# One load, one exponential and one signal per chunk instead of four, in the prompt's state scan

## The chip, the cores and the metric

The kernel runs on one core of a Trainium2 chip. The metric is the device time of one execution in microseconds. Three runs of the kernel before took 2939.79, 2950.26 and 2951.13 us; their median is 2950.26 us. The profile was taken of one execution of 2939.79 us.

## The reference, cut to what matters

The program is one inference step of a decoder layer: latent attention and a Mamba-2 scan side by side, then a mixer that gathers expert rows. The change lies in the scan over the prompt (512 tokens, 32 heads of 64 channels in 4 groups, state size 128), which goes in 4 chunks of 128 tokens:

```python
def step(h, inp):
    xc, dtc, bc, cc = inp
    acs = jnp.cumsum(dtc * a_gr, axis=1)
    seg = acs[:, :, None] - acs[:, None, :]
    decay = jnp.exp(jnp.where(causal[None, :, :, None, None], seg, -jnp.inf))
    cb = jnp.einsum('bign,bjgn->bijg', cc, bc)
    w = cb[..., None] * decay * dtc[:, None]
    y_diag = jnp.einsum('bijgr,bjgrp->bigrp', w, xc)
    y_off = jnp.einsum('bign,bgrpn->bigrp', cc, h) * jnp.exp(acs)[..., None]
    to_end = jnp.exp(acs[:, -1:] - acs) * dtc
    h_new = jnp.exp(acs[:, -1])[..., None, None] * h + jnp.einsum('bjgn,bjgr,bjgrp->bgrpn', bc, to_end, xc)
    return h_new, y_diag + y_off
```

So a chunk needs, for each of 32 heads, a 128 x 128 matrix of decays, and the state that the chunk before left.

## The kernel before, in words

The program is a row of stages, one function each. Each stage has its own block of five engine programs, whose order is the order of the code; engines wait for one another by counting semaphores, and a barrier ends a block. `prompt_scan` is one such stage. It does two things at once.

The first is the scan. The cumulative sums `acs` (32 heads x 512 tokens) lie in device memory. For each chunk c they are loaded to the tile `ce`, [128 partitions, 32 heads, 128 tokens], every partition getting the same values: 2 MB, in rows of 512 B. From then on:

- VectorE (DVE), L1260: `seg` = min(`ce` − `acs_tok`, 0), 32 instructions, one per head.
- ScalarE (ACT), L1224: `seg` = exp(`seg`); L1226 and L1227 two small ones; L1230: `ce` = exp(`ce`).
- DVE, L1267: `cb`, the masked products of B and C, then L1273: `seg` = `seg` * dt * `cb`, 32 instructions; L1280: `ce` = `ce` * C (not in chunk 0, which has no state before it).
- TensorE (PE), L1183 and L1185: Y of a head from `x_tok` and `seg`, and from `state` and `ce`. After each group of eight heads PE raises `summed`.
- DVE, L1287: `xw`; L1292: adds the skip term to Y; L1298 and L1303: the new state, from PE's products L1191.

`ce` is read by PE until the last product of its group of heads is summed; then ACT issues the load of the next chunk's values (L1236). The first chunk's load is issued by SyncE (L1135). All of these go in four quarters of eight heads (q or g from 0 to 3), each with its own load, wait and signal.

The second thing is filler: 16 products of 128 columns of a weight with all tokens, the gates (`gates(n)`, four per chunk), each 48 matmuls. SyncE loads a weight chunk, GpSimd (POOL) rounds it (L372), DVE makes the rest `w_lo` (L348), PE multiplies (L354 to L356), ACT drains the bank (L1209) and stores it (L1211). On PE two gate products stand between the first products of a chunk (`cb`) and Y, one between Y and the state's products L1191, one after these. Tokens and `cb` of the next chunk follow (L1166, L1170).

Of the kernel before, what the change touches and what calls it, by code (L numbers as in the profile page):

```python
# [19 lines left out]
ALU = mybir.AluOpType  # L20
ACT = mybir.ActivationFunctionType
# [3 lines left out]
P = 128  # L25
# [12 lines left out]
DI, HD, SH, G, N = 2048, 64, 32, 4, 128  # L38
# [1032 lines left out]
def prompt_scan(nc, A, K, S, h_hi, h_lo, proj, acs_dram, outs):  # L1071
# [4 lines left out]
    HP = SH // G  # L1076
    GATES = 2 * D // P
    EACH = GATES // TT
    with ExitStack() as ctx:
        m = Mem(nc, ctx, "scn")  # L1080
# [9 lines left out]
        seg, ce = m.sb("seg", [P, SH, P]), m.sb("ce", [P, SH, P])  # L1090
# [3 lines left out]
        state_out = xw[:, 0:1024].rearrange("p (b n) -> p b n", b=2)  # L1094
        to_end, end = m.sb("to_end", [P, SH]), m.sb("end", [P, SH])
        bank = [m.ps(f"bank{b}", [P, 512]) for b in range(4)]
        read_in = [m.sem(f"read_in{q}") for q in range(4)]
        turned, copied, cb_made = m.sem("turned"), m.sem("copied"), m.sem("cb_made")
        cb_masked, seg_made, decayed, exped, weighted = (m.sem(n) for n in ("cb_masked", "seg_made", "decayed", "exped", "weighted"))
        ce_made, x_weighted, summed, y_done, grown, state_done = (m.sem(n) for n in ("ce_made", "x_weighted", "summed", "y_done", "grown", "state_done"))  # L1100
        end_exped, end_in, chain = m.sem("end_exped"), m.sem("end_in"), m.sem("chain")
# [28 lines left out]
        @block.sync  # L1130
        def _(sp):
            columns = chunks_from(IN - 2 * D, GATES)
            weights_in(sp, w, w_view, w_in, lowered, columns, 0, 2)
            for q in range(4):
                sp.dma_start(heads_of(ce, q), acs_all[:, q * HP:(q + 1) * HP, 0:P].to_broadcast([P, HP, P])).then_inc(read_in[q], 16)  # L1135
            weights_in(sp, w, w_view, w_in, lowered, columns, 2, GATES)
            for q in range(4):
                sp.wait_ge(out_copied, q + 1)
                sp.dma_start(outs["ssm_p"][0, 0].rearrange("(k a) p n -> (a p) k n", a=2)[:, 4 * q:4 * q + 4, :],
                             state_out[:, q % 2, :].rearrange("p (k n) -> p k n", k=4)).then_inc(stored[q % 2], 16)  # L1140
            sp.wait_ge(stored[0], 32)
            sp.wait_ge(stored[1], 32)
# [59 lines left out]
        @block.scalar  # L1202
        def _(act):
            def drain(n):

                act.wait_ge(multiplied, n + 1)
                if n >= 2:
                    act.wait_ge(out_stored[n % 2], 16 * (n // 2))
                act.activation(out[:, n % 2].rearrange("p (s t) -> p s t", s=2), ps[:, n % 2, :, 0:HALF], ACT.Copy).then_inc(drained, 1)  # L1209
                act.wait_ge(drained, n + 1)  # L1210
                act.dma_start(proj[C_GA + n], out[:, n % 2]).then_inc(out_stored[n % 2], 16)  # L1211

            for c in range(TT):

                for q in range(5):
                    act.wait_ge(turned, 5 * c + q + 1)
                    if c and q == 0:
                        act.wait_ge(summed, 4 * c)
                        act.wait_ge(x_weighted, c)
                        act.wait_ge(grown, 4 * c)  # L1220
                    act.activation(x_tok[:, q * 512:(q + 1) * 512] if q < 4 else b_tok[:, :], bank_of(c, TOKENS + q)[:, :], ACT.Copy).then_inc(copied, 1)
                for q in range(4):
                    act.wait_ge(seg_made, 4 * c + q + 1)
                    act.activation(heads_of(seg, q), heads_of(seg, q), ACT.Exp).then_inc(decayed, 1)  # L1224
                act.wait_ge(end_in, c + 1)
                act.activation(to_end[:, :], to_end[:, :], ACT.Exp).then_inc(end_exped, 1)  # L1226
                act.activation(end[:, :], ce[:, :, P - 1], ACT.Exp).then_inc(end_exped, 1)  # L1227
                act.wait_ge(end_exped, 2 * c + 2)
                for q in range(4):
                    act.activation(heads_of(ce, q), heads_of(ce, q), ACT.Exp).then_inc(exped, 1)  # L1230
                drain(EACH * c)
                drain(EACH * c + 1)
                if c + 1 < TT:
                    for q in range(4):
                        act.wait_ge(summed, 4 * c + q + 1)
                        act.dma_start(heads_of(ce, q), acs_all[:, q * HP:(q + 1) * HP, (c + 1) * P:(c + 2) * P].to_broadcast([P, HP, P])).then_inc(read_in[q], 16)  # L1236
                drain(EACH * c + 2)
                drain(EACH * c + 3)
            for b in range(2):
                act.wait_ge(out_stored[b], 16 * (GATES // 2))  # L1240

        @block.vector
        def _(dve):
# [10 lines left out]
            lower_to(2)  # L1254
            for c in range(TT):
                at = slice(c * P, (c + 1) * P)
                for q in range(4):
                    dve.wait_ge(read_in[q], 16 * c + 16)
                    for h in range(8 * q, 8 * q + 8):
                        last = dve.tensor_scalar(seg[:, h, :], ce[:, h, :], S["acs_tok"][:, c, h:h + 1], 0.0, ALU.subtract, ALU.min)  # L1260
                    last.then_inc(seg_made, 1)
                dve.tensor_tensor(to_end[:, :], ce[:, :, P - 1], S["acs_tok"][:, c, :], ALU.subtract).then_inc(end_in, 1)
                lower_to(EACH * c + 3)
                dve.wait_ge(cb_made, c + 1)
                if c:
                    dve.wait_ge(weighted, 4 * c)
                dve.tensor_tensor(cb[:, :, :], bank_of(c, CB)[:, :].rearrange("p (g i) -> p g i", g=G),  # L1267
                                  K["keep"][:, :].rearrange("p (a i) -> p a i", a=1).to_broadcast([P, G, P]), ALU.mult).then_inc(cb_masked, 1)
                dve.wait_ge(cb_masked, c + 1)
                for q in range(4):  # L1270
                    dve.wait_ge(decayed, 4 * c + q + 1)
                    for h in range(8 * q, 8 * q + 8):
                        last = dve.scalar_tensor_tensor(seg[:, h, :], seg[:, h, :], S["dt_tok"][:, c, h:h + 1], cb[:, h // HP, :], ALU.mult, ALU.mult)  # L1273
                    last.then_inc(weighted, 1)
                    if q == 2:
                        lower_to(EACH * c + 4)
                if c:
                    for g in range(G):
                        dve.wait_ge(exped, 4 * c + g + 1)
                        dve.tensor_tensor(heads_of(ce, g), heads_of(ce, g),  # L1280
                                          S["x"][:, XC_ + g:XC_ + g + 1, at].to_broadcast([P, HP, P]), ALU.mult).then_inc(ce_made, 1)
                else:
                    dve.sem_inc(ce_made, G)
                dve.wait_ge(end_exped, 2 * c + 2)
                then(dve.tensor_tensor(to_end[:, :], to_end[:, :], S["dt_tok"][:, c, :], ALU.mult))
                dve.wait_ge(copied, 5 * c + 4)
                dve.tensor_tensor(xw[:, :].rearrange("p (h d) -> p h d", h=SH), x_tok[:, :].rearrange("p (h d) -> p h d", h=SH),  # L1287
                                  to_end[:, :].rearrange("p (h a) -> p h a", a=1).to_broadcast([P, SH, HD]), ALU.mult).then_inc(x_weighted, 1)
                for q in range(4):
                    dve.wait_ge(summed, 4 * c + q + 1)  # L1290
                    for k in range(4 * q, 4 * q + 4):
                        last = dve.scalar_tensor_tensor(S["x"][:, k, at], S["x"][:, k, at], S["skip"][:, k:k + 1],  # L1292
                                                        bank_of(c, Y + q)[:, (k % 4) * P:(k % 4 + 1) * P], ALU.mult, ALU.add)
                    last.then_inc(y_done, 1)
                lower_to(EACH * c + 5)
                view = lambda ap: ap.rearrange("p (h d) -> p h d", d=HD)
                if c:
                    then(dve.tensor_tensor(view(state[:, :]), view(state[:, :]),  # L1298
                                           end[:, :].rearrange("p (h a) -> p h a", a=1).to_broadcast([P, SH, HD]), ALU.mult))
                for g in range(G):  # L1300
                    dve.wait_ge(grown, 4 * c + g + 1)
                    part, new = state[:, g * 512:(g + 1) * 512], bank_of(c, GROWTH + g)[:, :]
                    (dve.tensor_tensor(part, part, new, ALU.add) if c else dve.tensor_copy(part, new)).then_inc(state_done, 1)  # L1303
                lower_to(EACH * c + 6)
# [1336 lines left out]
```

## Time and profile before

| what | before |
|---|---|
| median of three runs | 2950.26 us |
| the profiled execution | 2939.79 us |
| its span in the trace | 2937.8 us |
| busy, share of the span | PE 85%, DVE 70%, POOL 48%, ACT 30% |

The span is from the first to the last instruction of the profiled execution. The busy share of an engine is an average over stages with different limits. The prompt's scan lies between about 475 and 660 us of the span; a timeline lists the instructions of one engine in order of time there, and in brackets how long the engine had stood idle before one, and what released it. In waits, "issue" means that the profile shows nothing that the engine waited for.

### The profile page before, as it was taken

How to read it: one execution, taken by the hardware profiler on the slowest of the kernel's cores; microseconds unless marked ns; L12 is line 12 of the kernel's file. 1: busy time of each engine (PE TensorE's matmuls, PEld its weight loads, DVE VectorE, ACT ScalarE, POOL GpSimd, SP SyncE). 2: the span in 40 equal slices, each digit the busy share in tenths (PEclk: the TensorE clock that was granted, in tenths of full speed). 3: DMA queues.
4: the chain of work that ended last, by engine and by line, in shares of the span. 5: the costliest groups of instructions: out<-in, count | busy, mean ns of one | idle time of the engine just before them, and what ended most of it. 6: DMA issues, size and time to landing. Idle time of an engine off the chain costs nothing.

```text
span 2937.8 us, 36561 instructions
## 1 busy us (share of the span) xinstructions
PE 2486.9 (85%) x11667; PEld 1705.1 (58%) x11667; DVE 2054.1 (70%) x4001; ACT 885.7 (30%) x3576; POOL 1400.3 (48%) x1162
## 2 busy tenths in 40 slices
PE   3898997984998997887999999999999999846823
PEld 1898996873455563444666556565556565524810
DVE  3575686975460111498898989898989798976577
ACT  2232002314150000223454445454444444410110
POOL 0211232200000000287778788877787787765475
PEclk7899998997999998898999999999999999956555
DMA  4333575436006641699999999999999999999588
GB/s 152 99 97 109 177 219 165 127 89 201 15 1 186 223 140 64 240 398 393 373 345 394 337 395 352 381 362 376 377 356 381 357 370 360 384 356 379 204 314 322
DMA packets 372174, 776.19 MB, mean 264 GB/s; under 512 B 47250, under 2 KB 178323, under 8 KB 371946
## 3 DMA queue, kind: packets, MB, share of 16 engines
q0 software_dynamic: 154144, 562.17, 51.0%
q1 hardware_dynamic: 196714, 187.06, 19.9%
q10 hardware_dynamic: 21124, 24.63, 2.6%
q8 instruction: 93, 1.52, 0.2%
q14 instruction: 99, 0.80, 0.1%
HBM read 744.46 MB, written 29.50 MB: 263 GB/s over the span
## 4 chain that ended last, share of the span: by engine, by line
issue 25%; POOL 11%; DVE 8%; PE 8%; DMA 7%; ACT 1%; SPq 0%; POOLq 0%; DVEq 0%; ACTq 0%
POOL mix_v L2012 5%; POOL mix_u L2003 5%; DMA mix_u<-in_peer_u,mix_ids 4%; DVE mix_u L2485 3%; DVE mix_acc L2390 3%; PE mix_pair L2179 2%; PE mix_pair L2038 1%; DMA smp_w_out<-in_peer_keys 1%; PE mix_pair L2070 1%; PE mix_pair L2150 1%; PE mix_pair L2093 1%; PE mix_pair L2157 0%; DMA pag_kpe<-in_cache_kpe 0%; PE mix_pair L2085 0%; ACT L2288 0%
## 5 line engine op out<-in xcount | busy, mean ns | idle before, releaser
L2070 PE MATMUL mix_pair<-pag_wx,pag_ckvT 128*128 128x384 f32 (+3 forms) x3072 | 968.2, 462 | 14.4 <-ACT mix_raw L2252 9.4
L2485 DVE CUSTOM_DVE_ANT_0 mix_u<-mix_u,mix_h 128x1024 f32<-128x1024 f32 x512 | 623.3, 1217 | 216.7 <-DMA mix_u<-in_peer_u,mix_ids 214.6
L2012 POOL DMA_INDIRECT mix_v<-in_peer_v,mix_ids x512 | 644.1, 1258 | 224.3 <-issue 157.8
L2070 PEld LDWEIGHTS mix_pair<-pag_wx,pag_ckvT 128*128 128x128 f32 x3072 | 565.7, 192 | 304.8 <-issue 33.0
L2003 POOL DMA_INDIRECT mix_u<-in_peer_u,mix_ids x512 | 599.5, 1171 | 256.2 <-issue 147.7
L2390 DVE SCALAR_TENSOR_TENSOR mix_acc<-mix_v,mix_coef,mix_acc 128x1024 f32<-128x1024 f32 x449 | 575.1, 1281 | 0.0
L2250 ACT ACTIVATE mix_pair<-mix_pair 128x128 f32<-128x128 f32 x1024 | 267.1, 261 | 230.1 <-PE mix_pair L2070 229.3
L2085 PE MATMUL mix_pair<-mix_v,mix_diag 128*128 128x512 f32 x236 | 128.6, 672 | 103.7 <-ACT mix_diag L2267 102.7
L1988 POOL IOTA mix_count_i<- 128x16 int32 x1 | 0.1, 134 | 452.6 <-POOLq L88 452.6
L2259 ACT ACTIVATE mix_coef<-mix_dots 128x4 f32<-128x4 f32 x128 | 26.3, 205 | 550.8 <-DVE mix_dots L2485 550.8
L2250 ACT ACTIVATION_READ_ACCUMULATOR mix_pair<-mix_pair 128x1 f32 x1024 | 189.9, 185 | 0.0
L354 PE MATMUL stp_ps<-inp_h_hi,stp_w_hi 128*128 128x260 f32 x512 | 148.4, 290 | 17.3 <-DVE stp_w_lo L348 17.3
L356 PE MATMUL stp_ps<-inp_h_hi,stp_w_lo 128*128 128x260 f32 x512 | 146.3, 286 | 0.0
L355 PE MATMUL stp_ps<-inp_h_lo,stp_w_hi 128*128 128x260 f32 x512 | 145.9, 285 | 0.0
L1663 DVE TENSOR_TENSOR mrg_gate<-mrg_psB,mrg_gate 128x520 f32<-128x520 f32 x8 | 5.6, 699 | 197.4 <-PE mrg_psB L1624 197.4
L2085 PEld LDWEIGHTS mix_pair<-mix_v,mix_diag 128*128 128x128 f32 x236 | 47.9, 211 | 153.7 <-issue 82.5
L354 PE MATMUL cnv_ps<-inp_h_hi,cnv_w_hi 128*128 128x260 f32 x416 | 120.6, 290 | 0.0
L356 PE MATMUL cnv_ps<-inp_h_hi,cnv_w_lo 128*128 128x260 f32 x416 | 118.2, 284 | 0.0
L355 PE MATMUL cnv_ps<-inp_h_lo,cnv_w_hi 128*128 128x260 f32 x416 | 117.8, 283 | 0.0
L1624 PE MATMUL mrg_psB<-frt_x,mrg_wb 128*128 128x260 f32 x512 | 114.2, 384 | 0.0
L2038 PE MATMUL mix_pair<-chs_h2T,chs_wq 128*128 128x512 f32 x256 | 113.1, 600 | 0.4 <-ACT chs_h2T L2223 0.4
L354 PEld LDWEIGHTS stp_ps<-inp_h_hi,stp_w_hi 128*128 128x128 f32 x512 | 98.2, 192 | 19.3 <-DVE stp_w_lo L348 19.2
(480 smaller groups left out, 4210.9 us busy)
## 6 DMA issues: line engine op xcount, KB each, us to landing
pag_ckv<-in_cache_ckv SPq DMA_DIRECT2D x128, 256.0 KB, 14.8
stp_w<-in_w_in SPq DMA_DIRECT2D x32, 512.0 KB, 4.7
mrg_w_ada<-in_w_ada SPq DMA_DIRECT2D x8, 2048.0 KB, 8.2
cnv_w<-in_w_in SPq DMA_DIRECT2D x26, 512.0 KB, 3.5
keep_proj<-stp_out ACTq DMA_DIRECT2D x32, 260.0 KB, 2.8
ada_w_ada<-in_w_ada SPq DMA_DIRECT2D x4, 2048.0 KB, 11.3
stp_st<-in_state_ssm POOLq DMA_DIRECT2D x8, 1024.0 KB, 6.9
out_ssm_s<-stp_st POOLq DMA_DIRECT2D x8, 1024.0 KB, 6.9
```

What stands on the lines that cost most here:

```text
L354: pe.matmul(out, w_hi, x_hi, start=first, stop=False)
L355: pe.matmul(out, w_hi, x_lo, start=False, stop=False)
L356: return pe.matmul(out, w_lo, x_hi, start=False, stop=last)
L1624: last = pe.matmul(psB[:, b, s, 0:HALF], wb[:, b, k, :], yT[:, k, s * HALF:(s + 1) * HALF], start=(k == 0), stop=(k == KI - 1))
L2003: pool.indirect_dma_start(u[:, x % UR, :], None, u_rows, bass.IndirectOffsetOnAxis(at, 0)).then_inc(u_in[x % UR], 16)
L2012: pool.indirect_dma_start(v[:, y % VR, :], None, v_rows, bass.IndirectOffsetOnAxis(at, 0)).then_inc(v_in[y % VR], 16)
L2038: last = pe.matmul(bank[2 + side][:, :], wq[:, h % 2, k, side * P:(side + 1) * P], h2T[:, k, :], start=(k == 0), stop=(k == KD - 1))
L2070: last = pe.matmul(to, ckvT[:, g % 2, k, :], wx[:, k, lo:hi], start=(k == 0), stop=(k == KL - 1))
L2085: last = pe.matmul(psV[:, c, :], diag[:, d % 2, :], v[:, r, c * 512:(c + 1) * 512], start=(x == first_on_pe[t]), stop=(x == last_on_pe[t]))
L2250: last = act.activation(psN[j][:, at:at + NOPE], psN[j][:, at:at + NOPE], ACT.Square, accum_out=ss[:, b % 2, t, h:h + 1])
L2390: dve.scalar_tensor_tensor(acc[:, :], v[:, r, :], c, acc[:, :], ALU.mult, ALU.add).then_inc(v_used[r], 1)
L2485: dve.tensor_tensor_reduce(u[:, r, :], u[:, r, :], h2[:, t % 2, :], 1.0, 0.0, ALU.mult, ALU.add, dots[:, t % 2, slot:slot + 1]).then_inc(u ...
```

## The change

The quarters of the loads, of the first signal and of the exponentials become one each. The weighting L1273 and the products L1280 are still signalled to PE by groups of eight heads.

```diff
-        read_in = [m.sem(f"read_in{q}") for q in range(4)]
-        turned, copied, cb_made = m.sem("turned"), m.sem("copied"), m.sem("cb_made")
+        read_in, turned, copied, cb_made = m.sem("read_in"), m.sem("turned"), m.sem("copied"), m.sem("cb_made")
...
-            for q in range(4):
-                sp.dma_start(heads_of(ce, q), acs_all[:, q * HP:(q + 1) * HP, 0:P].to_broadcast([P, HP, P])).then_inc(read_in[q], 16)
+            sp.dma_start(ce[:, :, :], acs_all[:, :, 0:P].to_broadcast([P, SH, P])).then_inc(read_in, 16)
...
-                for q in range(4):
-                    act.wait_ge(seg_made, 4 * c + q + 1)
-                    act.activation(heads_of(seg, q), heads_of(seg, q), ACT.Exp).then_inc(decayed, 1)
+                act.wait_ge(seg_made, c + 1)
+                act.activation(seg[:, :, :], seg[:, :, :], ACT.Exp).then_inc(decayed, 1)
...
-                for q in range(4):
-                    act.activation(heads_of(ce, q), heads_of(ce, q), ACT.Exp).then_inc(exped, 1)
+                act.activation(ce[:, :, :], ce[:, :, :], ACT.Exp).then_inc(exped, 1)
...
-                    for q in range(4):
-                        act.wait_ge(summed, 4 * c + q + 1)
-                        act.dma_start(heads_of(ce, q), acs_all[:, q * HP:(q + 1) * HP, (c + 1) * P:(c + 2) * P].to_broadcast([P, HP, P])).then_inc(read_in[q], 16)
+                    act.wait_ge(summed, 4 * c + 4)
+                    act.dma_start(ce[:, :, :], acs_all[:, :, (c + 1) * P:(c + 2) * P].to_broadcast([P, SH, P])).then_inc(read_in, 16)
...
-                for q in range(4):
-                    dve.wait_ge(read_in[q], 16 * c + 16)
-                    for h in range(8 * q, 8 * q + 8):
-                        last = dve.tensor_scalar(seg[:, h, :], ce[:, h, :], S["acs_tok"][:, c, h:h + 1], 0.0, ALU.subtract, ALU.min)
-                    last.then_inc(seg_made, 1)
+                dve.wait_ge(read_in, 16 * c + 16)
+
+                for h in range(SH):
+                    last = dve.tensor_scalar(seg[:, h, :], ce[:, h, :], S["acs_tok"][:, c, h:h + 1], 0.0, ALU.subtract, ALU.min)
+                last.then_inc(seg_made, 1)
...
+                dve.wait_ge(decayed, c + 1)
                 for q in range(4):
-                    dve.wait_ge(decayed, 4 * c + q + 1)
...
                 if c:
+                    dve.wait_ge(exped, c + 1)
                     for g in range(G):
-                        dve.wait_ge(exped, 4 * c + g + 1)
```

On ACT this is what stands in chunk 0 before, from the exponential of `seg` to the reload of `ce` for chunk 1. In brackets is the semaphore that the instruction waits for:

```order
L1224 ACTIVATE scn_seg<-scn_seg 128x1024 [waits scn_seg_made] x4
L1226 ACTIVATE scn_to_end<-scn_to_end 128x32 [waits scn_end_in]
L1227 ACTIVATE scn_end<-scn_ce 128x32
L1230 ACTIVATE scn_ce<-scn_ce 128x1024 [waits scn_end_exped]
L1230 ACTIVATE scn_ce<-scn_ce 128x1024 x3
L1209 ACTIVATE scn_out<-scn_ps 128x520 [waits scn_multiplied]
L1211 DMA keep_proj<-scn_out 128x520 [waits scn_drained]
L1209 ACTIVATE scn_out<-scn_ps 128x520 [waits scn_multiplied]
L1211 DMA keep_proj<-scn_out 128x520 [waits scn_drained]
L1236 DMA scn_ce<-keep_acs 128x8x128 [waits scn_summed] x4
```

And in the changed kernel, whose lines have other numbers:

```order
L1221 ACTIVATE scn_seg<-scn_seg 128x4096 [waits scn_seg_made]
L1223 ACTIVATE scn_to_end<-scn_to_end 128x32 [waits scn_end_in]
L1224 ACTIVATE scn_end<-scn_ce 128x32
L1226 ACTIVATE scn_ce<-scn_ce 128x4096 [waits scn_end_exped]
L1207 ACTIVATE scn_out<-scn_ps 128x520 [waits scn_multiplied]
L1209 DMA keep_proj<-scn_out 128x520 [waits scn_drained]
L1207 ACTIVATE scn_out<-scn_ps 128x520 [waits scn_multiplied]
L1209 DMA keep_proj<-scn_out 128x520 [waits scn_drained]
L1231 DMA scn_ce<-keep_acs 128x32x128 [waits scn_summed]
```

Each row of four is one row of four times the size. The single load waits until all four groups of heads are summed.

On DVE, the differences of chunk 1 and what follows them up to the first weighting, before:

```order
L1260 TENSOR_SCALAR scn_seg<-scn_ce,frt_acs_tok 128x128 [waits scn_read_in0]
L1260 TENSOR_SCALAR scn_seg<-scn_ce,frt_acs_tok 128x128 x7
L1260 TENSOR_SCALAR scn_seg<-scn_ce,frt_acs_tok 128x128 [waits scn_read_in1]
L1260 TENSOR_SCALAR scn_seg<-scn_ce,frt_acs_tok 128x128 x7
L1260 TENSOR_SCALAR scn_seg<-scn_ce,frt_acs_tok 128x128 [waits scn_read_in2]
L1260 TENSOR_SCALAR scn_seg<-scn_ce,frt_acs_tok 128x128 x7
L1260 TENSOR_SCALAR scn_seg<-scn_ce,frt_acs_tok 128x128 [waits scn_read_in3]
L1260 TENSOR_SCALAR scn_seg<-scn_ce,frt_acs_tok 128x128 x7
L1262 TENSOR_TENSOR scn_to_end<-scn_ce,frt_acs_tok 128x32
L348 TENSOR_TENSOR scn_w_lo<-scn_w,scn_w_hi 128x1024 [waits scn_rounded]
L1267 TENSOR_TENSOR scn_cb<-scn_bank,frt_keep 128x512 [waits scn_weighted,scn_cb_made]
L1273 SCALAR_TENSOR_TENSOR scn_seg<-scn_seg,frt_dt_tok,scn_cb 128x128 [waits scn_decayed,scn_cb_masked]
```

The same place in the changed kernel:

```order
L1255 TENSOR_SCALAR scn_seg<-scn_ce,frt_acs_tok 128x128 [waits scn_read_in]
L1255 TENSOR_SCALAR scn_seg<-scn_ce,frt_acs_tok 128x128 x31
L1257 TENSOR_TENSOR scn_to_end<-scn_ce,frt_acs_tok 128x32
L348 TENSOR_TENSOR scn_w_lo<-scn_w,scn_w_hi 128x1024 [waits scn_rounded]
L1262 TENSOR_TENSOR scn_cb<-scn_bank,frt_keep 128x512 [waits scn_weighted,scn_cb_made]
L1268 SCALAR_TENSOR_TENSOR scn_seg<-scn_seg,frt_dt_tok,scn_cb 128x128 [waits scn_decayed,scn_cb_masked]
L1268 SCALAR_TENSOR_TENSOR scn_seg<-scn_seg,frt_dt_tok,scn_cb 128x128 x23
```

DVE's instructions keep their number, size and order; only the waits moved, to the first of 32.

## Rows read from the trace of the kernel before

**Rows 1.** Waits, 470 to 665 us: who waited for what, us in total, times, longest.
```profile
PE scn_bank L1183 <- issue: 10.9, 1, 10.9
DVE scn_state L1303 <- PE scn_bank L1191: 9.8, 13, 3.6
DVE scn_seg L1260 <- DMA scn_ce<-keep_acs: 7.1, 4, 2.5
```

**Rows 2.** Timeline of DVE, chunk 0: start, us, line, op, tiles, [idle before].
```profile
495.30 1.66 DVE L1260 TENSOR_SCALAR scn_seg<-scn_ce,frt_acs_tok 128x128 f32<-128x128 f32 x8 [2.18 <-DMA scn_ce<-keep_acs]
...
500.70 0.68 DVE L1267 TENSOR_TENSOR scn_cb<-scn_bank,frt_keep 128x512 f32<-128x512 f32 x1
501.42 6.44 DVE L1273 SCALAR_TENSOR_TENSOR scn_seg<-scn_seg,frt_dt_tok,scn_cb 128x128 f32<-128x128 f32 x24
```

**Rows 3.** Timeline of DVE, chunks 1 to 3.
```profile
526.64 8.00 DVE L1260 TENSOR_SCALAR scn_seg<-scn_ce,frt_acs_tok 128x128 f32<-128x128 f32 x32
...
536.53 6.39 DVE L1273 SCALAR_TENSOR_TENSOR scn_seg<-scn_seg,frt_dt_tok,scn_cb 128x128 f32<-128x128 f32 x24
...
546.86 4.62 DVE L1280 TENSOR_TENSOR scn_ce<-scn_ce,frt_x 128x1024 f32<-128x1024 f32 x4
...
568.26 8.07 DVE L1260 TENSOR_SCALAR scn_seg<-scn_ce,frt_acs_tok 128x128 f32<-128x128 f32 x32
...
608.42 8.07 DVE L1260 TENSOR_SCALAR scn_seg<-scn_ce,frt_acs_tok 128x128 f32<-128x128 f32 x32
```

**Rows 4.** Timeline of PE: first product of Y, and first gate product after.
```profile
513.84 0.58 PE L354 MATMUL scn_ps<-inp_h_hi,scn_w_hi 128*128 128x260 f32 x1
...
548.33 0.70 PE L1183 MATMUL scn_bank<-scn_seg,scn_x_tok 128*64 128x128 f32 x4 [2.75 <-DVE scn_ce L1280]
...
557.01 0.39 PE L354 MATMUL scn_ps<-inp_h_hi,scn_w_hi 128*128 128x260 f32 x1
...
575.46 0.37 PE L354 MATMUL scn_ps<-inp_h_hi,scn_w_hi 128*128 128x260 f32 x1
...
590.03 0.45 PE L1183 MATMUL scn_bank<-scn_seg,scn_x_tok 128*64 128x128 f32 x4 [2.82 <-DVE scn_ce L1280]
...
597.19 0.39 PE L354 MATMUL scn_ps<-inp_h_hi,scn_w_hi 128*128 128x260 f32 x1
```

**Rows 5.** Loads of ce: chunk 1's first, its fourth, chunk 0's four; issue, landing.
```profile
L1236 ACTq DMA_DIRECT2D scn_ce<-keep_acs x1: 377/377/377, 551.9 to 551.9; - x1
DMA to landing us min/median/max: 5.6/5.6/5.6
...
L1236 ACTq DMA_DIRECT2D scn_ce<-keep_acs x1: 1839/1839/1839, 557.1 to 557.1; - x1
DMA to landing us min/median/max: 12.2/12.2/12.2
...
L1135 SPq DMA_DIRECT2D scn_ce<-keep_acs x4: 875/2058/4145, 476.0 to 481.1; - x4
DMA to landing us min/median/max: 7.8/11.6/14.2
```

**Rows 6.** Exponentials: timeline of ACT, and L1224 by ns min/median/max.
```profile
534.20 3.93 ACT L1224 ACTIVATE scn_seg<-scn_seg 128x1024 f32<-128x1024 f32 x4
...
L1224 ACT ACTIVATE scn_seg<-scn_seg x16: 1056/1089/1096, 485.5 to 618.8; 128x1024 f32<-128x1024 f32 x16
```

**Rows 7.** DMA issues of the page: KB each, median us to landing.
```profile
mrg_w_ada<-in_w_ada SPq DMA_DIRECT2D x8, 2048.0 KB, 8.2
```

**Rows 8.** Timeline of PE, in an earlier stage.
```profile
253.52 0.59 PE L354 MATMUL stp_ps<-inp_h_hi,stp_w_hi 128*128 128x260 f32 x1 [9.31 <-DVE stp_w_lo L348]
```

**Rows 9.** Windows: length, busy PE, PEld, DVE, ACT, POOL; PEclk; DMA; GB/s.
```profile
253.00:258.00 5.00, 4.48 (x21) 4.48 (x22) 2.69 (x4) 1.48 (x3) 2.28 (x2) 0.51 0.58 165
258.00:263.00 5.00, 5.00 (x44) 5.00 (x43) 4.93 (x3) 0.60 (x1) 1.17 (x2) 1.00 0.16 48
```

**Rows 10.** Timeline of ACT, drain of a gate product in chunk 1.
```profile
563.09 0.60 ACT L1209 ACTIVATE scn_out<-scn_ps 128x520 f32<-128x520 f32 x1 [16.86 <-PE scn_ps L356]
```

## The prediction

> **What bounds the kernel now.** The page's busy shares come first (they are in the table of the profile above): over the whole run no engine is full, so the shares say nothing of one stage. The change lies in one stage, the prompt's state scan, which the timelines put at about 475 to 660 us; so I read that stretch alone, first its waits, then the order in time of VectorE (DVE), TensorE (PE) and ScalarE (ACT).
>
> The waits [rows 1] show that DVE waits little: 7.1 us for the loads of `ce`, all in the first chunk, and 9.8 us for PE's state products. PE waits 10.9 us once (chunk 0) and then at most 2.8 us per chunk, until DVE has made `ce`. DVE's timeline says the same: the decay differences (L1260) start at 526.64, 568.26 and 608.42 [rows 3], so a chunk takes 41.6 and 40.2 us, and in between DVE is nearly never idle. The ring that sets the end of the stage is therefore: differences, weighting (L1273), `ce` times C (L1280) on DVE; then Y (L1183/L1185), a gate product and the state products on PE; then the state on DVE; then the next differences. The exponentials on ACT and the reload of `ce` by DMA lie beside this ring. What must be seen is how much room each of them has.
>
> *The reload.* In chunk 1 four quarters are issued, as each group of heads is summed: the first at 551.9, to land 5.6 us later, at 557.5, the fourth at 557.1, to land 12.2 us later, at 569.3 [rows 5]. So they arrive one every 3.93 us. The first reader starts at 568.26 with no wait, and needs the fourth quarter only 6 us later. *The exponentials.* Four pieces of 1024 take 3.93 us together, from 534.20 [rows 6], while DVE is still at the differences and at other work; the weighting starts at 536.53, about 1.9 us after the last difference (526.64 + 8.00) [rows 3].
>
> **The change part by part.** It computes the same; each group of four (loads, difference signals, exponentials) becomes one. Instructions on DVE and PE are the same ones in the same order. What changes is when they may start.
>
> *a) Exponential of `seg` after all 32 differences (four times).* It can only begin when the 32nd difference is done, and no weighting can begin until all of it is done. Chunk 0: the fourth group of differences begins at 495.30, since the fourth quarter lands there [rows 2]. One load of the same bytes lands at the same moment, and then all 32 differences stand behind it: 8.00 us [rows 3], to 503.3. The exponential: I take the 3.93 us of the four (bounds: 3.6, if three fixed parts go, and 4.4 for four times the single 1.09) [rows 6], to 507.2. The weighting started at 501.42, so chunk 0 is late by 5.8 us. In chunks 1 to 3, once the differences have started, it costs 8.00 + 3.93 − (536.53 − 526.64) = 2.0 us each. DVE's other work there (`to_end`, a w_lo and the mask of `cb`, the 1.9 us between 534.64 and 536.53) fits below the 3.93.
>
> *b) Reload of `ce` after the last sum, in one transfer (three times).* The load is issued when Y ends, not after its first quarter. Its length is not in the trace: no 2 MB load with this source was run. From the quarters: first one 5.6, three more at 3.93, so 5.6 + 11.8 = 17.4 us. Upper bound: in chunk 0 the four, issued together, took from 476.0 to 481.1 + 14.2, 19.3 us, with weights ahead of them [rows 5]. Lower bound: the 2 MB loads of w_ada land in 8.2 us [rows 7]. I take 17.4, since it is the same source, destination and row of 512 B, and the four already ran back to back.
>
> *c) PE's clock.* PE will stand before each Y. The row nearest to what comes is the 9.31 us idle before 253.52 [rows 8]: granted clock 0.51 (1.2 GHz) for the next 5 us, then 1.00 [rows 9]. Of 4.48 us of work at half clock half is lost, 2.2 us. Y takes 7.2 us at full clock (590.03 to 597.19) [rows 4], so 9.4 us here. Bounds: no loss, or all of Y at half clock, 14.4.
>
> The sum, chunk by chunk:
> - Chunk 0: +5.8. Y ended at 513.84 [rows 4], now 519.6; the load lands at 537.0. DVE started at 526.64 and is ready at 532.4, so the start is +10.4; plus 2.0 by (a), weighting is at +12.4.
> - Chunk 1: Y starts at 548.33 + 12.4 = 560.7, ends at 570.1; `ce` lands at 587.5, where DVE began at 568.26: +19.2, weighting +21.2.
> - Chunk 2: Y starts at 590.03 + 21.2 = 611.2, ends 620.6; `ce` lands at 638.0, where DVE began at 608.42: +29.6, weighting +31.6.
> - Chunk 3: no reload. For Y's slower start +0.5 (0 if its clock had fallen before as well, as in chunk 1, where Y took 8.7 us; 2.2 if not). The rest of the stage follows as before.
>
> Together +32 us. By this, the ring becomes Y 9.4, load 17.4, differences 8.1, exponential 3.9, weighting and first `ce` product about 11.8 (536.53 to 548.33): 50.6 us where it was 41.6 and 40.2.
>
> *What costs nothing.* The `exped` wait: ACT's pass over `ce` has the size of that over `seg`, so it ends some 4.4 us after it (two small ones between); DVE's weighting takes 10.3 (536.53 to 546.86) [rows 3], so 5.9 us of cover are left. Fewer launches on ACT: it is idle for 16.86 us before its next drain [rows 10]. ACT's queue when it issues 2 MB: the fourth quarter held it for 1.84 us, as transfers stood ahead of it [rows 5]; one big issue may hold ACT for 7 us or so, at worst until the load has landed. Behind it waits the drain of gate chunk 4c+2, which before came 6.1 us after Y's end (563.09 against 557.01) [rows 4, 10], and whose bank PE wants only at 575.46, 18.4 us after Y's end; so up to 17.4 us nothing is late, and ACT's copies after that have slack until the differences are done. The three or four weight loads and the stores queue as before; the store of 4c+2 goes behind the load, and ACT asks for it only after the next exponentials. Nothing outside the stage is touched: the stages are parted by barriers.
>
> *Two rules against these rows.* The quarters carry 512 KB per 3.93 us, 133 GB/s [rows 5]. The Trainium skill ("DMA: Bandwidth & Descriptors", section Bandwidth, Measured) says to batch loads to at least 1 MiB, and its formula of 2.0 us plus bytes over 436 GB/s would give an estimated 6.8 us for the 2 MB; by that the reload would not be seen and the sum would be near +6. The trace disagrees: the three later quarters, already queued, came no faster than 3.93 us each. A rule of the Trainium skill that speaks against the change ("Perfetto Trace Analysis", Optimizing Scalar/DVE Operations): where ScalarE is not saturated but causes bubbles on others, smaller instructions may let work end sooner; grouping saves about 93 ns each. Here grouping would give back an estimated 1.1 us in all (4 × 3 × 93 ns), against +32.
>
> **The rivals.**
> 1. *The big load is quick: no measurable change.* A single transfer might run at the rate of the w_ada loads, 8.2 us [rows 7]. Then `ce` is there before DVE asks; the point from which this decides is 568.26 − 557.01 = 11.3 us (12.8 in chunk 0). Chunk 0 would gain what the earlier load gives, but the mask of `cb` stands behind a w_lo and begins at 500.70 [rows 2], so about 0; chunks 1 to 3 keep 2.0 each by (a): +6. For it: 512 KB in 3.93 us is half the rate of those loads, so there is room above it. Against it: the spacing of queued quarters. Between the ends, each us by which the load is under 17.4 takes off 3 us.
> 2. *PE stays at half clock through all of Y.* For it: after only 2.75 us of standing Y took 8.7 us in chunk 1 (548.33 to 557.01), against 7.2 in chunk 2 after 2.82 [rows 4]. Price: 14.4 − 9.4 = 5.0 us in each of chunks 1 to 3, as the load is issued only at Y's end: +15, so +47. The same time would come of a load that is 5 us slower beside the weights. Against it: 253 to 263, where dense work brought the clock back.
> 3. *The big load is a little quicker: +15 to +25.* In one piece it lands in 12 to 15 us, three times 2.4 to 5.4 us sooner.
>
> **How the numbers follow.** The profiled execution took 2939.8 us (span 2937.8); the median of the runs is 2950.3, so 10.5 above. With +32 it would be 2971.8, and against the median 2982.3. Forecast 65%, own range +26 to +39 (exponential −1 to +2, load from 15.4 to 19.3, clock −5 to +2), so 2976 to 2989. Rival 2: 13%, 2997. Rival 1: 11%, 2956. Rival 3: 8%, 2965 to 2975. Something that I don't see, 3%, faster. The runs of before lie 11 us apart, so I set the range from 2962 to 3000. What can be told from no change is about 0.5%, 15 us. Slower by more: forecast, rivals 2 and 3: 0.85. Same: rival 1 and the edge of 3: 0.12. Faster: 0.03.
>
> **What would show it.** In the changed profile: one load of `ce` per chunk that lands about 17 us after the end of Y; DVE waiting for it 4.6 us in chunk 1 and about 6 us in chunks 2 and 3; one exponential of 4096 in about 3.9 us, and the weighting starting right after it; PE standing 9 to 11 us before each Y, at granted clock 0.5 for the next 4 to 5 us; starts of the differences some 50 us apart; nothing moved in the later stages beyond a shift. I am wrong if the load lands within 11 us, if the weighting starts before the whole exponential, or if another stage changes by more than 5 us.

## The result and the profile after

| | before | after |
|---|---|---|
| median of the runs | 2950.7 us (4) | 2983.4 us (4) |
| profiled execution / its span | 2939.8 / 2937.8 us | 2975.7 / 2973.8 us |
| the stage | 188.1 us | 219.3 us |

The ratio of the runs is 1.0118 (the two medians alone give 1.0111), 95% interval 1.0098 to 1.0139: slower by 29 to 41 us of 2951. Forecast were +32 us and 2982. "The stage" is here, and in all of what follows, the time from PE's first product of the prompt's scan to the next stage's table load on ACT: 474.99 to 663.08 before, 476.95 to 696.25 after. The stage began 1.96 us later after the change, so times of after are compared with before less 1.96. The stage grew by 31.2 us; of the span's 36.0 the other 4.8 lie before and behind it (2.0 and 2.8), where both kernels are the same.

The timeline of DVE after the change, at the differences and the weighting of each chunk, answers to [rows 2, 3]:

```profile
496.67 8.07 DVE L1255 TENSOR_SCALAR scn_seg<-scn_ce,frt_acs_tok 128x128 f32<-128x128 f32 x32 [11.41 <-DMA scn_ce<-keep_acs]
508.51 7.17 DVE L1268 SCALAR_TENSOR_TENSOR scn_seg<-scn_seg,frt_dt_tok,scn_cb 128x128 f32<-128x128 f32 x24 [1.92 <-ACT scn_seg L1221]
538.60 8.07 DVE L1255 TENSOR_SCALAR scn_seg<-scn_ce,frt_acs_tok 128x128 f32<-128x128 f32 x32 [5.71 <-DMA scn_ce<-keep_acs]
550.45 7.20 DVE L1268 SCALAR_TENSOR_TENSOR scn_seg<-scn_seg,frt_dt_tok,scn_cb 128x128 f32<-128x128 f32 x24 [1.92 <-ACT scn_seg L1221]
589.63 7.82 DVE L1255 TENSOR_SCALAR scn_seg<-scn_ce,frt_acs_tok 128x128 f32<-128x128 f32 x32 [6.59 <-DMA scn_ce<-keep_acs]
601.23 7.17 DVE L1268 SCALAR_TENSOR_TENSOR scn_seg<-scn_seg,frt_dt_tok,scn_cb 128x128 f32<-128x128 f32 x24 [1.92 <-ACT scn_seg L1221]
640.47 8.00 DVE L1255 TENSOR_SCALAR scn_seg<-scn_ce,frt_acs_tok 128x128 f32<-128x128 f32 x32 [6.48 <-DMA scn_ce<-keep_acs]
652.25 6.39 DVE L1268 SCALAR_TENSOR_TENSOR scn_seg<-scn_seg,frt_dt_tok,scn_cb 128x128 f32<-128x128 f32 x24 [1.92 <-ACT scn_seg L1221]
```

Two new waits stand in each chunk: for the load before the differences, and 1.92 us for the exponential before the weighting. Between the last three starts of the differences lie 51.0 and 50.8 us, where it was 41.6 and 40.2. The loads in chunks 0 to 2, by issue and landing, answer to [rows 5]:

```profile
L1231 ACTq DMA_DIRECT2D scn_ce<-keep_acs x3: 377/378/380, 520.8 to 622.8; - x3
DMA to landing us min/median/max: 17.7/17.7/17.8
```

PE's first product of Y in chunks 1 to 3, with how long it stood, answers to [rows 4]:

```profile
562.28 0.70 PE L1181 MATMUL scn_bank<-scn_seg,scn_x_tok 128*64 128x128 f32 x4 [10.55 <-DVE scn_ce L1275]
...
613.03 0.70 PE L1181 MATMUL scn_bank<-scn_seg,scn_x_tok 128*64 128x128 f32 x4 [11.16 <-DVE scn_ce L1275]
...
663.26 0.70 PE L1181 MATMUL scn_bank<-scn_seg,scn_x_tok 128*64 128x128 f32 x4 [10.44 <-DVE scn_ce L1275]
```

The windows from there on in chunk 1 (the figure before the last two is the granted clock) answer to [rows 9]:

```profile
562.00:566.00 4.00, 3.72 (x36) 3.75 (x38) 4.00 (x5) 0.00 (x0) 3.39 (x1) 0.50 0.00 0
566.00:568.00 2.00, 2.00 (x31) 2.00 (x30) 1.97 (x2) 0.00 (x0) 0.37 (x1) 0.76 0.00 0
568.00:570.00 2.00, 2.00 (x42) 2.00 (x39) 2.00 (x7) 0.00 (x0) 0.00 (x0) 1.00 0.04 8
```

After 10.55 us of standing, some 5 us of Y run at half clock (1.2 GHz); Y lasts from 562.28 to the first gate product at 571.72, 9.44 us. In chunks 2 and 3 it lasts 9.65 and 8.46 us; before, the three took 8.68, 7.16 and 8.83.

### The profile page after: what moved, and what is told of

Its sections match the earlier page's. It is cut to its first block, busy times and chain, and to the rows that moved or that the text cites. A ratio compares the mean times of both kernels' runs of the same rounds, so it can differ in the third digit from the quotient of the medians.

```text
span 2973.8 us, 36525 instructions
## 1 busy us (share of the span) xinstructions
PE 2481.9 (83%) x11667; PEld 1702.0 (57%) x11667; DVE 2056.1 (69%) x4001; ACT 883.2 (30%) x3552; POOL 1386.6 (47%) x1162
## 4 chain that ended last, share of the span: by engine, by line
issue 26%; POOL 11%; DMA 9%; DVE 7%; PE 5%; ACT 1%; SPq 0%; POOLq 0%; DVEq 0%; ACTq 0%
DMA mix_u<-in_peer_u,mix_ids 6%; POOL mix_v L2007 6%; POOL mix_u L1998 5%; DVE mix_u L2480 3%; DVE mix_acc L2385 3%; PE mix_pair L2174 2%; PE mix_pair L2033 1%; DMA smp_w_out<-in_peer_keys 1%; PE mix_pair L2088 1%; PE mix_pair L2152 0%; DMA pag_kpe<-in_cache_kpe 0%; ACT L2283 0%; DMA mod_mul<-keep_ada 0%; PE mix_pair L2040 0%; DVE mix_rstd L2406 0%
```

## The experiments

Chips differ, and the rest of the program moves by more than most terms here (in the first four kernels that I changed, on a chip where the whole took some 3% longer, what follows the stage took 2367 to 2395 us). So the stage in the trace is what is compared. The third column leaves out chunk 0: it counts from the first weighting of chunk 0 to the end of the stage, because chunk 0 alone moved by 2 us between runs in which it was the same.

| kernel | stage, us | of it behind chunk 0's first weighting, us | ratio to before (95%) |
|---|---|---|---|
| before, twice | 188.1, 183.7 | 161.7, 158.9 | |
| changed, twice | 219.3, 219.0 | 187.7, 187.5 | 1.0118; 1.0115 (1.0084 to 1.0145) |
| exponentials whole | 193.1 | 167.5 | 1.0050 (1.0021 to 1.0079) |
| load whole | 213.8 | 184.2 | 1.0111 (1.0075 to 1.0147) |
| loads issued late | 190.6 | 166.2 | 1.0010 (0.9975 to 1.0046) |
| four loads, one wait | 211.8 | 181.5 | 1.0076 (1.0050 to 1.0102) |
| PE kept busy | 212.3 | 181.2 | 1.0076 (1.0051 to 1.0101) |
| other source | 200.4 | 169.2 | 1.0057 (1.0022 to 1.0091) |
| other pitch | 195.3 | 170.5 | one run |
| long rows, whole | 188.4 | 165.8 | 1.0017 (1.0002 to 1.0031) |
| long rows, quarters | 174.9 | 156.6 | 0.9973 (0.9957 to 0.9989) |

The kernel before and the changed one, run once more on one chip:

> The kernel before once more, for its trace on the same chip as the runs beside it. From the first product of the stage on PE to the next stage's table load on ACT it took 188.1 us; expected 188 to 190 us here.

> The changed kernel once more, beside the kernel before on the same chip: its stage took 219.3 us in the first trace, 31.2 us more than before. By the theory (the parts add up along the ring) the same 30 to 33 us here, wherever the rest of the program stands; if the loss depends on the chip or on the load of its memory, the load of ce lands more than 1 us away from 17.7 us.

The loads landed in 17.8 to 18.0 us and the changed stage took the same time within 0.3 us. The kernel before took 4.4 us less than in its first trace: 1.7 of it up to the first weighting of chunk 0, and 1.7 because Y ran into the half clock in one chunk and not in two: 8.62 us in chunk 2 there, 8.68 and 8.83 in chunks 1 and 3 in the first trace, at a granted clock of 0.57 to 0.62 in the first 4 us, and 7.16 at 1.00 in the others. So its stage is known to 4 us, and the loss is 31 to 35 us.

**The parts one by one.** First the exponentials alone: against the kernel before,

```diff
                 for q in range(4):
                     dve.wait_ge(read_in[q], 16 * c + 16)
...
-                    last.then_inc(seg_made, 1)
+                last.then_inc(seg_made, 1)
...
-                    act.wait_ge(seg_made, 4 * c + q + 1)
-                    act.activation(heads_of(seg, q), heads_of(seg, q), ACT.Exp).then_inc(decayed, 1)
+                act.wait_ge(seg_made, c + 1)
+                act.activation(seg[:, :, :], seg[:, :, :], ACT.Exp).then_inc(decayed, 1)
```

> The changed kernel with its loads in four quarters again, each issued and waited for as before; the differences are still signalled once and the two exponentials are one instruction each. Theory (the two parts of the change add up along the ring, each by its own wait): chunk 0 pays nothing, since the last difference ends at about 497.0, the exponential of 3.6 us ends at 500.6 and the mask of cb is not made before 501.4; chunks 1 to 3 pay 8.0 + 3.6 + 0.1 - 9.9 = 1.8 us each: +5.5 us, 2956 us. The weighting starts right after the exponential, with DVE idle 1.9 us before it. Rival (most of the loss is in the coarse exponential, for example because PE then stands and its clock falls): +15 us or more.

```profile
524.50 8.07 DVE L1258 TENSOR_SCALAR scn_seg<-scn_ce,frt_acs_tok 128x128 f32<-128x128 f32 x32
536.34 7.18 DVE L1271 SCALAR_TENSOR_TENSOR scn_seg<-scn_seg,frt_dt_tok,scn_cb 128x128 f32<-128x128 f32 x24 [1.92 <-ACT scn_seg L1223]
```

These are differences and weighting of chunk 1: 11.84 us apart, where it was 9.89. The stage took 193.1 us, +5.0 on the first trace of before (+9.4 on the second). The run times say more, +6 to +24 us; since the changed lines end with the stage, and what follows it differs by up to 27 us between kernels that are the same there, I go by the stage, and the rest of that ratio stays unexplained. Then the load alone, the change with its exponentials in quarters again:

> The changed kernel with the differences signalled and the exponentials done in four quarters again; the load stays whole. Theory: chunk 0 starts its differences when the whole load lands and its mask of cb follows them, +4.1 us; each reload lands 17.7 us after the end of Y: weighting at +9.0, +16.2, +25.0 us in chunks 1, 2, 3, so +25.5 us in all, 2976 us. DVE waits for the load 5 to 7 us in each of chunks 1 to 3. Rival (the coarse exponential carries the loss): under +15 us.

213.8 us, +25.8 against the 25.5 forecast; the load is the larger part. DVE waited 5.8, 7.8 and 7.4 us for it, a little over the 5 to 7 said, as the loads landed in 18.1 to 18.9 us on this chip. That 5.0 + 25.8 = 30.8 leaves only 0.4 of the 31.2 is in part chance, as the first weightings of chunk 0 show, here with the exponentials whole and then with the load whole:

```profile
501.79 6.39 DVE L1271 SCALAR_TENSOR_TENSOR scn_seg<-scn_seg,frt_dt_tok,scn_cb 128x128 f32<-128x128 f32 x24 [0.78 <-ACT scn_seg L1223]
...
507.47 6.39 DVE L1271 SCALAR_TENSOR_TENSOR scn_seg<-scn_seg,frt_dt_tok,scn_cb 128x128 f32<-128x128 f32 x24
```

From the start of the stage they come 0.9 us earlier and 3.2 us later than before, 2.3 together, where the change itself has 5.1: chunk 0 pays for the exponential only where the load is whole too. Behind that the two runs together have 5.9 + 22.5 = 28.4 us, where the change has 26.1. One reason is PE's clock, which the two parts don't pay twice: the three Y together take 27.7 us with the exponentials alone, 27.3 with the load alone and 27.6 with both, against 24.7 before; with the exponentials alone PE stood 3.9 to 4.7 us before each, and the granted clock began at 0.50 to 0.57.

**Which property of the load.** It was issued later, it was one transfer, and it had one wait. Against the kernel before, only issued later:

```diff
+                    act.wait_ge(summed, 4 * c + 4)
                     for q in range(4):
-                        act.wait_ge(summed, 4 * c + q + 1)
```

> The kernel before, but the four quarter loads of the next chunk are issued together after the last sum of Y, as late as the single load of the changed kernel; each still has its own semaphore and its own wait. Theory A (the loss comes from waiting for the last byte before the first difference): the first quarter lands 5.6 us after the end of Y, at 562.6, where DVE asks at 568.3; the fourth at 17.4 to 17.7, 574.5, where it is asked for at 574.3: +0 to +1 us, 2951 us. Theory B (the loss comes from issuing late, 5 us later than the first quarter was): about half of what the whole load cost, +10 to +20 us.

+2.5 us, within what before itself varies. The cover was thinner than counted: the timeline shows DVE waiting for a fourth quarter in each of chunks 1 to 3, 3.57 us at most,

```profile
500.96 6.45 DVE L1273 SCALAR_TENSOR_TENSOR scn_seg<-scn_seg,frt_dt_tok,scn_cb 128x128 f32<-128x128 f32 x24
...
568.58 4.87 DVE L1260 TENSOR_SCALAR scn_seg<-scn_ce,frt_acs_tok 128x128 f32<-128x128 f32 x24
577.02 1.66 DVE L1260 TENSOR_SCALAR scn_seg<-scn_ce,frt_acs_tok 128x128 f32<-128x128 f32 x8 [3.57 <-DMA scn_ce<-keep_acs]
```

but three quarters are worked on meanwhile, and the weighting comes 0.4, 2.0 and 0.4 us later after the first difference than before. The stage hides part of the price: chunk 0, which the edit doesn't touch, was 2.0 us shorter (first weighting at 500.96, 24.4 us into the stage, against 26.4). Behind it the stage took 4.6 us more than in the first trace of before and 7.3 more than in the second. So issuing late costs some 5 to 7 us: more than theory A's 0 to 1, less than theory B's 10 to 20. Now with the same four loads, and a wait for all of them first:

```diff
                 for q in range(4):
                     dve.wait_ge(read_in[q], 16 * c + 16)
+                for q in range(4):
                     for h in range(8 * q, 8 * q + 8):
```

> The kernel before, but the four quarter loads are issued together after the last sum of Y, and DVE waits for all four before its first difference; exponentials in quarters. It differs from the run that issued late only in the waits, and from the run with the whole load only in the size of the transfers. Theory (the wait for the last byte costs, not the size of the transfer): the stage takes as long as with the whole load, 213.8 us, within 2 us. Rival (one transfer of 2 MB is slower or faster than four of 512 KB): it differs by three times the difference, 5 us or more.

211.8 us: 21 us more than the run before it by the waits alone, 5.9 of them in chunk 0 and 15.3 behind it, and 2.1 from the run with one transfer, just over the 2 allowed and far from the rival's 5. So the loss by the load is mainly the wait for its last byte before the first difference; behind chunk 0 it is 15 of 20 to 23 us, and the late issue is the rest. The 2.1 us between one transfer and four are fewer than before itself varies by.

**PE's clock.** In the changed kernel, before Y in chunks 1 to 3:

```diff
+                if c:
+                    bank_free(pe, c, Y)
+                    for _i in range(80):
+                        pe.matmul(bank_of(c, Y)[:, 0:HALF], h_hi[:, 0, 0:P], h_hi[:, 0, 0:HALF], start=True, stop=True)
```

> The changed kernel with 80 matmuls of 128x260 more before Y in chunks 1 to 3, on fixed operands, into the bank that Y then overwrites: about 9.6 us of work at full clock in the 10.4 to 11.2 us that PE stood idle. Theory (c): Y starts at full clock and takes 7.2 us instead of 9.4 in each of the three chunks, all of it on the ring, so the stage falls from 219.2 us by 6 to 7, to 212.6. Rival 1 (the clock does not lie on the ring, since DVE's product of ce feeds Y no faster than 1.15 us a group): under 2 us. Rival 2 (the added matmuls end late and push Y): the stage grows.

212.3 us, 6.9 less. Y starts and ends, in chunk 1 of this kernel, at

```profile
559.52 0.45 PE L1185 MATMUL scn_bank<-scn_seg,scn_x_tok 128*64 128x128 f32 x4 [2.10 <-DVE scn_ce L1279]
...
566.68 0.39 PE L354 MATMUL scn_ps<-inp_h_hi,scn_w_hi 128*128 128x260 f32 x1
```

7.16 us for 9.44, and 7.16 in chunks 2 and 3 too, so the half clock at Y's start is on the ring and its price is that of the forecast. This is the price against a PE that never stands. Against the kernel before, whose Y ran into the half clock in two chunks of three, the three Y of the change took 27.6 us for 24.7: the clock accounts for 2.9 of the 31 us.

**Why the load takes 17.7 us.** First another source, in the changed kernel:

```diff
-                    act.dma_start(ce[:, :, :], acs_all[:, :, (c + 1) * P:(c + 2) * P].to_broadcast([P, SH, P])).then_inc(read_in, 16)
+                    act.dma_start(ce[:, :, :], A["w_in"][:, 0:P, 0:8192].rearrange("l p (h a n) -> p (l h) a n", a=2, n=P)[:, :, 0, :]).then_inc(read_in, 16)
```

> The changed kernel, but the three reloads of ce read rows of a weight matrix in place of acs: the same 4096 rows of 512 B to the same place, every partition from its own row, so that no source byte is read twice (chunks 1 to 3 compute with other numbers, and to_end takes its difference the other way round there). Theory A (the load is slow because all 128 partitions read the same 16 KB): it lands in 8 to 10 us after its issue, DVE does not wait for it, and what is left is chunk 0 and the exponentials, +11 us, 2962 us. Theory B (512 B rows through one queue go at about 3.9 us per 1024, whatever they read): it lands in 17.7 us and the time is 2983 us.

As many rows of 512 B came in 9.5 to 11.2 us, and DVE waited for no reload; the stage, 200.4 us, was 12.3 over before, where 11 was forecast:

```profile
L1231 ACTq DMA_DIRECT2D scn_ce<-in_w_in x3: 390/390/393, 520.9 to 609.3; - x3
DMA to landing us min/median/max: 9.5/11.2/11.2
```

By its outcome this spoke for theory A, 128 readers of the same bytes. But the edit changed two things: the rows of a partition also lie 1 KB apart there, not 2 KB. The next run kept the readers and changed how the bytes lie:

```diff
-("acs", (SH, TP), F32)
+("acs", (TT, SH, P), F32)
...
-act.dma_start(ce[:, :, :], acs_all[:, :, (c + 1) * P:(c + 2) * P].to_broadcast([P, SH, P])).then_inc(read_in, 16)
+act.dma_start(ce[:, :, :].rearrange("p h t -> p (h t)"), acs_all[c + 1:c + 2, :].to_broadcast([P, SH * P])).then_inc(read_in, 16)
```

(parts of lines; the store of acs and the first load follow the new order).

> The changed kernel with acs stored chunk by chunk, so that the whole load reads 16 KB in one piece per partition instead of 32 rows of 512 B; all 128 partitions still read the same 16 KB. The run with another source landed in 9.5 to 11.2 us, so the shared source matters. Theory A (what is slow is that the same bytes are served 128 times): it still lands in about 17.7 us and the stage stays at +31 us. Theory B (what is slow is the number of requests for the same rows; long requests are served as fast as others): it lands in 8 to 10 us, DVE waits for no reload, chunk 0 starts some 8 to 10 us earlier, and what is left of the change is the exponentials: the stage at +0 to +4 us against before.

It lands in 7.2 to 7.4 us, and the stage is at 188.4: +0.3 against the first trace of before, +4.7 against the one from the same chip, so at the 0 to +4 us of theory B or just over:

```profile
L1231 ACTq DMA_DIRECT2D scn_ce<-keep_acs x3: 326/326/327, 510.3 to 597.9; - x3
DMA to landing us min/median/max: 7.2/7.3/7.4
```

So sharing the bytes is not by itself what is slow, and theory A fell. Left were the short rows and their pitch of 2 KB. The last run has short rows again, the same for all, at 640 B:

```diff
-("acs", (SH, TP), F32)
+("acs", (TT, SH, 160), F32)
...
-acs_all[:, :, (c + 1) * P:(c + 2) * P].to_broadcast([P, SH, P])
+acs_all[c + 1:c + 2, :, 0:P].to_broadcast([P, SH, P])
```

(parts of lines again).

> The changed kernel with acs stored chunk by chunk, each head's 512 B at a pitch of 640 B instead of 2 KB; the load is again 32 rows of 512 B per partition, the same for all partitions. Theory A (what is slow is many short reads of the same few rows): it lands in 16 to 18 us, the stage near 219 us. Theory B (the 2 KB pitch is what made it slow, by sending the rows to the same part of the memory): it lands in 7 to 11 us, the stage near 188 us.

```profile
L1231 ACTq DMA_DIRECT2D scn_ce<-keep_acs x3: 377/377/379, 512.3 to 600.6; - x3
DMA to landing us min/median/max: 10.7/10.8/11.0
```

10.8 us, by size, count and readers the load that takes 17.7. The stage, 195.3, is over the 188 that I gave for it, and 7.0 over the run in long rows, whose exponentials are just as whole. In chunk 0 it loses 2.3: the first load lands in 11.9 us, not 9.7, and DVE stands 4.54 us for it, not 2.26. The other 4.7 lie behind chunk 0, and no run takes them apart; this kernel ran only once, on another chip. What the pitch does inside the memory no run shows, nor whether a pitch of 2 KB is slow also when each partition reads its own bytes.

**A version that beats both.** The kernel before, in quarters, with acs stored chunk by chunk:

> The kernel before with the same layout of acs: quarters in pieces of 4 KB per partition. Theory A: as before, 188 us for the stage. Theory B: the reloads were hidden already, so only chunk 0 gains: its quarters land one every 2 us or less, the weighting starts at about 493 instead of 501.4 and the stage is 6 to 9 us shorter than before, about 180 us, a faster kernel by 0.2 to 0.3%.

```profile
485.41 8.09 DVE L1260 TENSOR_SCALAR scn_seg<-scn_ce,frt_acs_tok 128x128 f32<-128x128 f32 x32
495.39 6.39 DVE L1273 SCALAR_TENSOR_TENSOR scn_seg<-scn_seg,frt_dt_tok,scn_cb 128x128 f32<-128x128 f32 x24
```

Its stage began 2.06 us later than in the first trace of before, so the weighting of chunk 0 stands at 493.3 there, 8.1 us earlier [rows 2], and the differences run through without a wait. The stage is 174.9 us, 9 to 13 less, and the ratio 0.9973, with its interval, lies wholly under 1. The theory gave the gain to chunk 0 alone. Behind it the stage is 2 to 5 us shorter as well: the differences of chunks 1 to 3 take 7.21 us there, where they took 8.0 to 8.1. Why they do, no run shows.

## Why the prediction was right

- *What bounds.* The ring through DVE, PE and the reload. Each added wait on it came out in the stage, chunk by chunk as below. The forecast was for the kernel before as in its first trace; its second is 4.4 us shorter, so that stage and forecast agree within 1 us (+31.2 for +32) is closer than the traces can bear out, and in part luck.
- *a) The exponential.* Forecast 2.0 us per chunk, measured 550.45 − 538.60 = 11.85 from differences to weighting against 9.89 [rows 3], 1.96; 1.6 and 1.8 in chunks 2 and 3. Two small errors met: the whole one takes 3.6 us, not 3.93, and two hand-offs of 0.1 us weren't counted. The 1.1 us that fewer launches were to give back counted the exponentials of `seg` alone; the same working with those of `ce` gives 2.2. Each whole one saved 0.3 us of ACT, and that of `ce` is off the ring. Chunk 0: +5.8 forecast, 508.51 − 1.96 − 501.42 = +5.1 measured.
- *b) The load.* 17.4 us forecast, 17.7 measured. That four queued quarters tell the speed of one transfer was the assumption that carried the forecast; the run with four loads and one wait bears it out: in chunk 1 its first difference comes 18.3 us after the end of Y, and 19.1 us after it in the run with the load whole.
- *c) The clock.* Y of 9.4 us forecast, 9.44 and 9.65 in chunks 1 and 2, but 8.46 in chunk 3, 0.4 less than before, where +0.5 stood; 2.2 us a chunk against full clock forecast, 6.9 us for three by the run with the added matmuls.
- *Chunk by chunk.* The weighting was to be late by 12.4, 21.2 and 31.6 us; measured, less 1.96, 12.0, 21.1 and 31.9. PE stood 10.4 to 11.2 us, within the 9 to 11 said but for 0.2; DVE waited 5.7, 6.6 and 6.5 for the load, where 4.6, 6 and 6 stood.
- *A step that was wrong, and cost nothing.* I had ACT held for some 7 us by the one big issue. It was held 0.38 us; the next store's issue was held instead:

```profile
571.82 0.38 ACTq L1231 DMA_DIRECT2D scn_ce<-keep_acs  x1
577.78 0.60 ACT L1207 ACTIVATE scn_out<-scn_ps 128x520 f32<-128x520 f32 x1 [21.96 <-PE scn_ps L356]
578.41 3.41 ACTq L1209 DMA_DIRECT2D keep_proj<-scn_out  x1
```

- *The rivals.* The quick load (rival 1) doesn't happen with this source. Where the layout was changed and the load did come in 7.3 us, the stage was at +0.3 to +4.7, not +6. The rival gave chunk 0 no gain, since the mask of `cb` stands behind a w_lo; but with the quick load that w_lo came earlier too, 18.8 us into the stage and not 24.6, and the weighting 3.9 us earlier. Rival 2, all of Y at half clock: 5 us of it were. The fit of the Trainium skill ("DMA: Bandwidth & Descriptors", Anatomy of one DMA — SWDGE (gpsimd) path), made on transfers issued from GpSimd, gives an estimated 6.8 us for 2 MB. The loads here were issued by ACT: the one in long rows, 7.3 us, agrees with it within 0.5 us, and the one in rows of 512 B at 2 KB, 17.7 us, does not.

## What to carry to other kernels

Before merging waits, compare for each the time at which the first piece is needed with the time at which the last one lands: here 11.3 against 17.7 us after the end of Y, and that difference was paid in every turn of the loop. How late a transfer may be issued and how finely it is waited for are two questions: behind chunk 0 the first cost some 5 to 7 us, the second 15. When two parts of a change are tried one by one, compare them chunk by chunk and not by the sum alone: here the sum fitted within 0.4 us by two misfits of over 2 us that cancelled. When a load is slower than others of its size, change how its source lies before cutting or merging it.

## What the runs showed of the hardware that I had not expected

The same 2 MB to the same place, in one transfer, landed in 17.7 us from 32 rows of 512 B at a pitch of 2 KB, in 10.8 us from such rows at 640 B, in 9.5 to 11.2 us from 4096 different rows, and in 7.3 us from 16 KB in one piece, read by all 128 partitions in every case but the third. I had laid the speed to the readers and then to the length of the rows; with the readers as they were, the pitch alone was worth 7 us, and one piece in place of the short rows 3.5 more. The 4096 different rows lay at a pitch of 1 KB within a partition, so that run does not tell readers from pitch.
